# Branch order, interleaved opening of the output projection, and router products of unnormalised tokens in a two-block fp32 kernel

## The reference, cut to what matters

```python
h = rms_norm(x, norm_mix) * (1 + scale_m) + shift_m
proj = h @ w_in
y_a, y_b, y_c = mamba2(...), stick_breaking(...), gated_deltanet(...)      # 256 x 512 each
branch_proj = einsum("bsie,ied->bsid", [y_a, y_b, y_c], w_branch)          # three products, 512 -> 1024
gates = sigmoid(br_gate)                                                   # three slices of proj, 1024 wide
merged = sum(gates * branch_proj, axis=2)
x = x + gate_m * (merged @ w_out)                                          # "the projection" below
h = rms_norm(x, norm_ffn) * (1 + scale_f) + shift_f
logits = h @ [w_group | w_router] + [b_group | b_router]                   # 4 + 32 columns
# top group, then two of its eight experts; SwiGLU experts: (silu(xi @ w_gate) * (xi @ w_up)) @ w_down
x = x + gate_f * hier_moe(h, ...)
```

## Time and profile before

| what | value |
|---|---|
| median of 3 runs | 1608.63 us (1608.3 to 1609.04) |
| the profiled execution | 1611.41 us |
| its span, first to last instruction | 1609.6 us |
| mean granted TensorE clock | 0.96 of full |
| busy: PE, DVE, ACT, POOL | 1499.6, 780.5, 571.4, 294.6 us |
| HBM read | 373.35 MB, 233 GB/s over the span |

### The profile page before, as it was taken

One profiled execution on the slowest core, in us unless ns is written; L12 is line 12 of the kernel. 1 busy time (PEld: TensorE's weight loads), 2 busy tenths in 40 slices (PEclk: granted clock), 3 DMA queues, 4 the chain that ended last, 5 costly groups with the idle time before them and its releaser, 6 DMA issues.

```text
span 1609.6 us, 28268 instructions
## 1 busy us (share of the span) xinstructions
PE 1499.6 (93%) x11238; PEld 1252.1 (78%) x11238; DVE 780.5 (48%) x1411; ACT 571.4 (35%) x895; POOL 294.6 (18%) x121
## 2 busy tenths in 40 slices
PE   7978999999999999999998988978799999999897
PEld 5857999999868999989997977978566665555554
DVE  4963888648674888434543524552422222111212
ACT  2245545454345555356553115433111111101101
POOL 0021112212201212227760002672000000000000
PEclk9989999999999999989999987998899999999999
DMA  7674555664434555625541212463899999999995
GB/s 289 235 275 146 168 169 169 195 235 153 137 134 134 182 185 180 199 92 163 172 144 40 66 40 77 168 239 129 327 424 425 427 428 430 426 427 427 428 427 227
DMA packets 64609, 375.82 MB, mean 233 GB/s; under 512 B 7296, under 2 KB 7552, under 8 KB 49152
## 3 DMA queue, kind: packets, MB, share of 16 engines
q1 hardware_dynamic: 64512, 374.43, 61.9%
HBM read 373.35 MB, written 1.05 MB: 233 GB/s over the span
## 4 chain that ended last, share of the span: by engine, by line
PE 62%; issue 13%; DMA 11%; DVE 8%; SPq 2%; ACT 2%; POOL 1%; POOLq 0%; DVEq 0%; ACTq 0%
PE lin L673 8%; PE lin L675 8%; PE lin L674 8%; DMA modrow<-in_experts 7%; PE mixp L1292 4%; PE mixp L1296 4%; PE stat L1317 4%; DVE mixers L1933 3%; PE lin L692 2%; DMA moe_low<-in_experts 2%; DMA moe_high<-in_experts 2%; DVE cat L2117 1%; PE stat L1260 1%; PE stat L673 1%; PE mixp L673 1%
## 5 line engine op out<-in xcount | busy, mean ns | idle before, releaser
L673 PE MATMUL lin<-r_hi,w_hi 128*128 128x256 f32 x1464 | 428.7, 293 | 14.9 <-POOL w_lo L1737 5.1
L674 PE MATMUL lin<-r_lo,w_hi 128*128 128x256 f32 x1464 | 418.5, 286 | 0.0
L675 PE MATMUL lin<-r_hi,w_lo 128*128 128x256 f32 x1464 | 418.4, 286 | 0.0
L673 PEld LDWEIGHTS lin<-r_hi,w_hi 128*128 128x128 f32 x1464 | 285.4, 195 | 23.0 <-POOL w_lo L1737 6.7
L674 PEld LDWEIGHTS lin<-r_lo,w_hi 128*128 128x128 f32 x1464 | 285.6, 195 | 0.9
L675 PEld LDWEIGHTS lin<-r_hi,w_lo 128*128 128x128 f32 x1464 | 285.2, 195 | 0.0
L1741 POOL TENSOR_TENSOR w_lo<-ring,w_hi 128x1024 fp32r<-128x1024 f32 x71 | 175.4, 2483 | 236.2 <-ACT w_hi L1358 235.8
L1770 DVE TENSOR_TENSOR w_lo<-ring,w_hi 128x1024 fp32r<-128x1024 f32 x126 | 156.5, 1246 | 85.3 <-ACT w_hi L1364 65.2
L1737 POOL TENSOR_TENSOR w_lo<-ring,w_hi 128x1024 fp32r<-128x1024 f32 x42 | 108.3, 2578 | 481.7 <-ACT w_hi L1364 298.4
L1364 ACT ACTIVATE w_hi<-ring 128x1024 fp32r<-128x1024 f32 x124 | 129.6, 1048 | 57.4 <-PE mixp L675 48.5
L1358 ACT ACTIVATE w_hi<-ring 128x1024 fp32r<-128x1024 f32 x119 | 124.0, 1049 | 35.4 <-PE lin L675 17.4
(11 more groups left out here) (460 smaller groups left out, 2834.0 us busy)
## 6 DMA issues: line engine op xcount, KB each, us to landing
ring<-in_panels SPq DMA_DIRECT2D x272, 512.0 KB, 3.6
moe_high<-in_experts SPq DMA_DIRECT2D x32, 2048.0 KB, 30.0
...
```

The costliest lines, as they stand in the source:

```text
L673: pe.matmul(o, w_hi[:, slot, c], r[0], start=start, stop=False, skip_group_check=True)
L674: pe.matmul(o, w_hi[:, slot, c], r[1], start=False, stop=False, skip_group_check=True)
L675: return pe.matmul(o, w_lo[:, slot, c], r[0], start=False, stop=stop, skip_group_check=True)
```

## The change

1. Branch 1 now has the order that branch 0 has: product, gate, gate, four times. `is_gate`, the index of a gate, `gate_branch` and the layout in HBM follow; ACT's `round_merged` calls move among the gates.
2. The projection opens with two panels interleaved tile by tile (`opening`).
3. The router's products use x, not h: `route(m)` multiplies tile m of x with router weights that DVE has scaled by the gain (L2359 of the changed kernel), in [36, 256] form, one in each panel of the projection from the third on. The shift's part is made once by PE (eight products of `mod` broadcast, L1253) and added to the bias row by DVE (L2358). After rs is there, DVE multiplies the 36 x 256 logits by it (L2379), PE turns them with two transposes (L1267), and the routing starts.
4. h is scaled by POOL (x * rs, L1778, eight tiles), ACT applies gain and shift in one operation.
5. Token pieces are turned in the order half 0 of both token tiles, then half 1; the four DVE subtractions stand behind the whole routing instead of in its middle. The fourth bank's zeros come behind the first gathering. `first_max` has one operation less.
6. DVE's `gate_branch(0, 3)` stands ahead of the norm of the gated branch, and ACT splits the second panel of branch 2 behind branch 0's last gates instead of before them.

```diff
@@ -365 +365 @@
-            return j % 3 != 0 if i == BRANCHES[0] else j < KD
+            return j < KD if i == 2 else j % 3 != 0
@@ -492 +492 @@
-        def turn_bank(g):
+        TURNS = ((0, 0), (1, 0), (0, 1), (1, 1))
@@ -494 +494,3 @@
-            return statbank(g - 1) if g in (1, 2) else mixbank(1)
+        def turn_bank(n):
+
+            return (mixbank(1), statbank(0), statbank(1), lin[3][:, :])[n]
@@ -745,0 +748,9 @@
+            def route(m):
+
+                if m == 0:
+                    pe.wait_ge(mod_read, 4)
+                mm = pe.matmul(mixbank(0)[0:36, 0:T], wsmall[:, m, 16:52], x[:, m, :], start=m == 0, stop=m == KD - 1,
+                               skip_group_check=True)
+                if m == KD - 1:
+                    mm.then_inc(ev("logits_ready"), 1)
+
@@ -748 +759,13 @@
-                for m in range(KD):
+                if first:
+                    opening = [split_panel(j) for j in range(2)]
+                    for b in opening:
+                        bank(b)
+                    for i in range(KD):
+                        pe.wait_ge(h_ready, seen(h_ready))
+                        for b in opening:
+                            mm = split_matmul(lin[b][:, 0:T], (b, slice(i * P, (i + 1) * P)), [t[:, i, :] for t in rows],
+                                              i == 0, i == KD - 1)
+                            if i == KD - 1:
+                                mm.then_inc(panel_done, 1)
+                    panels.advance(2)
+                for m in range(2 if first else 0, KD):
@@ -751 +774 @@
-                    split_linear(b, first and m == 0, rows)
+                    split_linear(b, False, rows)
@@ -754,0 +778,2 @@
+                        if first:
+                            route(m - 2)
@@ -756,0 +782,2 @@
+                    if first:
+                        route(m)
@@ -1019 +1046 @@
-                    if split and (i, j) in ((2, 1), (2, KD), (1, KD)):
+                    if split and (i, j) in ((2, 1), (2, KD), (1, 0)):
@@ -1223,0 +1251,5 @@
+            pe.wait_ge(mod_read, 3)
+            for k in range(KD):
+                mm = pe.matmul(mixbank(0)[:, 0:36], mod[:, 3 * KD + k:3 * KD + k + 1].to_broadcast([P, P]), wsmall[:, k, 16:52],
+                               start=k == 0, stop=k == KD - 1, skip_group_check=True)
+            mm.then_inc(mod_turned, 1)
@@ -1229,7 +1260,0 @@
-            for c in range(NT):
-                for i in range(KD):
-                    if c == 0:
-                        pe.wait_ge(h_ready, seen(h_ready))
-                    mm = pe.matmul(mixbank(0)[:, c * 36:(c + 1) * 36], h[:, i, c * P:(c + 1) * P], wsmall[:, i, 16:52],
-                                   start=i == 0, stop=i == KD - 1, skip_group_check=True)
-            mm.then_inc(ev("logits_ready"), 1)
@@ -1238,2 +1263 @@
-            for g in range(4):
-
+            for g in range(3):
@@ -1241,4 +1265,9 @@
-                if g == 3:
-                    pe.wait_ge(ev("ht_copied"), 1)
-                turned(turn_bank(g), [h[:, (g % 2) * 4 + j, (g // 2) * P:(g // 2 + 1) * P] for j in range(4)], ev("ht_turned"))
-            pe.wait_ge(ev("assigned"), 1)
+            pe.wait_ge(ev("routed"), 1)
+            for c in range(NT):
+                mm = pe.transpose(mixbank(0)[:, T + c * 36:T + (c + 1) * 36], e_hid[0:36, c * P:(c + 1) * P], K["ident"][0:36, 0:36])
+            mm.then_inc(ev("logits_ready"), 1)
+            for n, (c, half) in enumerate(TURNS):
+                if n % 2 == 0:
+                    pe.wait_ge(h_ready, seen(h_ready, 4))
+                turned(turn_bank(n), [h[:, half * 4 + j, c * P:(c + 1) * P] for j in range(4)], ev("ht_turned"))
+            pe.wait_ge(ev("routed"), 2)
@@ -1278,0 +1308 @@
+            pe.matmul(lin[3][:, :], e_turned[:, 0:P], cst[:, 0:512], start=True, stop=False, skip_group_check=True)
@@ -1563,2 +1593,4 @@
-                    act.activation(h[:, k, :], h[:, k, :], ACT.Identity, bias=shift)\
-                        .then_inc(r_hi_ready if half == 0 else h_ready, 1)
+                        act.activation(h[:, k, :], h[:, k, :], ACT.Identity, bias=shift).then_inc(r_hi_ready, 1)
+                    else:
+                        act.activation(h[:, k, :], h[:, k, :], ACT.Identity, bias=shift, scale=gains[:, KD + k:KD + k + 1])\
+                            .then_inc(h_ready, 1)
@@ -1587 +1619 @@
-                        u = 2 * (j // 3) + j % 3 - 1 if i == BRANCHES[0] else j
+                        u = j if i == 2 else 2 * (j // 3) + j % 3 - 1
@@ -1664 +1696 @@
-            split_hi(BRANCHES2 + 2)
+            split_hi(BRANCHES2 + 1)
@@ -1682,7 +1714,7 @@
-            gates(1, 0, 10)
-            round_merged(0, 2)
-            gates(1, 10, 11)
-            round_merged(1, 2)
-            gates(1, 11, 12)
-            round_merged(2, 2)
-            round_merged(3, 1)
+            gates(1, 0, 6)
+            round_merged(0, 6)
+            gates(1, 6, 9)
+            round_merged(1, 6)
+            gates(1, 9, 12)
+            round_merged(2, 6)
+            round_merged(3, 3)
@@ -1694 +1726,2 @@
-                act.activation(h_tm_hi[:, g // 2, (g % 2) * 512:(g % 2 + 1) * 512], turn_bank(g), ACT.Copy).then_inc(ev("ht_hi"), 1)
+                c, half = TURNS[g]
+                act.activation(h_tm_hi[:, c, half * 512:(half + 1) * 512], turn_bank(g), ACT.Copy).then_inc(ev("ht_hi"), 1)
@@ -1742,0 +1776,3 @@
+            pool.wait_ge(ev("routed"), 1)
+            for k in range(KD):
+                pool.tensor_tensor(h[:, k, :], x[:, k, :], rs[:, 0, :], ALU.mult).then_inc(ev("h_scaled"), 1)
@@ -2104,2 +2140,2 @@
-                first = i == BRANCHES[0]
-                if not first and pair == 0:
+                in_turn = i != 2
+                if not in_turn and pair == 0:
@@ -2110 +2146 @@
-                    panels.taken(1 + m if first else u - KD - pair)
+                    panels.taken(1 + m if in_turn else u - KD - pair)
@@ -2123 +2159 @@
-                panels.advance(3 if first else 1)
+                panels.advance(3 if in_turn else 1)
@@ -2288,0 +2325 @@
+            gate_branch(0, 3)
@@ -2294 +2330,0 @@
-            gate_branch(0, 3)
@@ -2319,0 +2356,5 @@
+            a0 = ROWS["b_route"][0]
+            dve.wait_ge(mod_turned, 4)
+            dve.tensor_tensor(rows[:, a0:a0 + 36], rows[:, a0:a0 + 36], mixbank(0)[:, 0:36], ALU.add)
+            dve.tensor_tensor(wsmall[:, :, 16:52], wsmall[:, :, 16:52], gains[:, KD:2 * KD].unsqueeze(2).broadcast_to([P, KD, 36]),
+                              ALU.mult).then_inc(mod_read, 1)
@@ -2332,3 +2372,0 @@
-            panels.settled()
-            modulated(KD)
-
@@ -2337,0 +2376 @@
+            panels.settled()
@@ -2339,2 +2378,4 @@
-            a0 = ROWS["b_route"][0]
-            link(dve.tensor_tensor(r_lg, mixbank(0)[:, 0:72].rearrange("p (c n) -> p c n", c=NT),
+            dve.wait_ge(rs_ready, seen(rs_ready))
+            dve.tensor_tensor(e_hid[0:36, :], mixbank(0)[0:36, 0:T], rs[0:36, 0, :], ALU.mult).then_inc(ev("routed"), 1)
+            dve.wait_ge(ev("logits_ready"), 2)
+            link(dve.tensor_tensor(r_lg, mixbank(0)[:, T:T + 72].rearrange("p (c n) -> p c n", c=NT),
@@ -2356,2 +2397 @@
-                link(dve.tensor_scalar(r_at, r_at, 1000.0, None, ALU.add))
-                link(dve.tensor_tensor(onehot, iota(n), wide(r_at, n), ALU.is_equal))
+                link(dve.tensor_tensor(onehot, onehot, wide(r_at, n), ALU.is_equal))
@@ -2362 +2402 @@
-                c, d = g // 2, slice((g % 2) * 512, (g % 2 + 1) * 512)
+                c, d = TURNS[g][0], slice(TURNS[g][1] * 512, (TURNS[g][1] + 1) * 512)
@@ -2369,2 +2408,0 @@
-            for g in range(3):
-                lower_tokens(g)
@@ -2385,3 +2423,4 @@
-            dve.tensor_tensor(assign, r_oh1, r_oh2, ALU.add).then_inc(ev("assigned"), 1)
-            lower_tokens(3)
-            dve.wait_ge(ev("assigned"), 1)
+            dve.tensor_tensor(assign, r_oh1, r_oh2, ALU.add).then_inc(ev("routed"), 1)
+            for g in range(4):
+                lower_tokens(g)
+            dve.wait_ge(ev("routed"), 2)
@@ -2497 +2536 @@
-        if i == 0:
+        if i != 2:
```

## The result

The changed kernel takes 1597.33 us in the median of 8 runs (1586.21 to 1599.94), the kernel before 1608.84 in 8 runs (1599.1 to 1610.95): ratio 0.993, 95% interval 0.9902 to 0.9957. That is 11.5 us less; 9.8 were forecast.

What follows compares the result with a forecast made beforehand. The DMA stream of expert weights bounds the last stage, so its start and holes set the end. Closing the hole (-7.7 us) and an earlier projection end (-2.05) gave -9.8: 1598.8 us, range 1594.5 to 1604.8.

Steps and rivals of the forecast that it cites:

- hole: Expert weight stream runs dry before expert 3's load, which waits for step 0; sized 7.7 us, forecast to close.
- (a) to (c): Up to branch 2's merges: PE stall removed, shift products added, router-weight scaling delays merges; together +1.3 us (-0.6 to +1.7).
- (d): Branch 1's new order: product banks come free slightly late at three places; +0.6 us (0 to 2.6).
- (e): PE's 7.39 us idle time between branch 1 and the projection shrinks; -5.5 us (-5.9 to -4.2).
- (f): Opening of the projection: first panel no longer slowed by the lower PE clock; -1.5 us.
- (g): Five router products on PE before the projection's last panel, 0.43 us each; +2.15 us.
- (h): Projection's first two panels end together, so the fourth panel's split is late; +0.9 us (0 to 1.8).
- The room: Step 0 reads its weights 32.5 us behind the projection's end, up to 36.5 with POOL/DVE contention; limit 37.5.
- 1: Rival: POOL slows both chains behind rs, step 0 through at +40 to +41.5; 2.5 to 4 us stall remains; 1602; chance 0.09.
- 2: Rival: PE's wait before the projection stays, last merges or c_hi still ending 7 us behind the products; 1605.9; chance 0.07.
- 4: Rival, slower: POOL's h tiles cost by the instruction, stream stalls 13.5 us instead of 7.7; 1612.4; chance 0.04.
- 3: Rival, more gained: no POOL-slowed scaling, no lower clock, no late fourth-panel split; projection -6 us; 1594.9; chance 0.10.

Runs made afterwards that it cites:

- seam_only: Kernel before with only branch 1 in the order product, gate, gate and the two-panel opening of the projection; 1598.99 us, ratio 0.9958 to the kernel before.
- routes_behind: Changed kernel with router products moved behind the projection's last sums and three banks' zeros placed among the turned tokens; 1585.45 us.

## Why the prediction came out as it did

**Right in kind.** The forecast's case came in: hole closed, seam shorter. By steps, forecast against measured, for the end of the projection:

| step | forecast | measured | from |
|---|---|---|---|
| (a) to (c) | +1.3 | +0.6 | opening, changed less seam_only |
| (d) | +0.6 | +0.2 | end of branch 1, seam_only less before |
| (e) | -5.5 | -5.7 | 7.39 against 1.66 |
| (f) | -1.5 | -1.9 | opening to stream, 27.05 against 28.18, less (h) |
| (g) | +2.15 | +3.0 | routes_behind |
| (h) | +0.9 | +0.8 | wait ahead of the fourth panel in seam_only |
| sum | -2.05 | -3.1 | stream |

The first two lines are at the size of the scatter of 0.5 us. That the sum is only 1.0 off is in part luck: (a) to (c) were forecast 0.7 too long and (g) 0.85 too short.

**(a) to (c).** The chain was right: y1's lower part comes 1.1 us earlier, then 0.18 for the bias and 2.55 for the scaling beside POOL (forecast 0.23 and 2.1), first merge 1.5 later. But it was carried through to the end at its full size, and only part arrived. In seam_only the merges start 1.86 us earlier than in the changed kernel, but the first five additions fall beside POOL and the first ten take 16.2 us; in the changed kernel two fall into POOL's pause and ten take 15.0. Of the 1.86 us 1.2 are won back there, and 0.6 arrive. The fourth panel of branch 1 was to come later than 1052.43: it came at 1052.30, from the mark 0.13 later.

**(g)** was mis-sized. A router product was priced as a sum over x, 0.43 us, and cost 0.75. From sum to sum a panel takes 4.05 us after (1097.89 to 1101.94 above), and before, in PE's order of time:

```profile
1096.84 0.59 PE L712 MATMUL stat<-sq,cst 128*128 128x256 f32 x2
...
1100.14 0.59 PE L712 MATMUL stat<-sq,cst 128*128 128x256 f32 x2
```

That is 3.30, so 0.75 more. Four such products are 3.0. The fifth, the first in time, lies in the wait for the fourth panel (h) and is free: 0.22 us of idle time are left of 0.78. The two steps share their place, and the prediction added them.

**The hole** was mis-sized: it was read as 7.7 us from the DMA share; by bytes it is 9.7, and 9.5 came back. The share of 0.88 over 1158 to 1165 went with 316 GB/s, so it should not have been taken at its face. This one term is most of what the total was short: 1.8 of 2.8 us from the mark.

**The room** was thought to be 5 us (32.5 against 37.5) and was 1.2 (33.9 against 35.1, both behind the projection's end). The forecast stood closer to the edge than it said: with its own 32.5 there would have been 2.6 us to spare, not 5, and the upper bound of its own contention term, +36.5, would have left 1.4 us of hole. That the hole closed whole was thus less certain than its "both ends lie below 37.5".

**Behind the projection**, +33.9 against +32.5. The tiles were 0.69 us each (guess 0.8), h was whole with ACT's part at +11.9 (+12.2). The routing took 8.44 us instead of 5.7: operations of 0.2 us take 0.45 to 0.74 there beside POOL's tiles, as the rows from 1118.70 on show, 2.7 us in all. The prediction had allowed for that with 4 us in its upper bound. That chain, not the tokens, ended last: PE's ranks wait for DVE's row at 1124.83, and the idle time ahead of them is 1.07.

**Rivals.** 1 and 2 are out by the traces. 4 is out: POOL's tile costs by its elements, a quarter of 2.48 plus 0.07. 3 came close in size, 12.5 us against its 13.7, but not by its path: the projection gave 3.1 of its 6, and the rest is the mis-sized hole. Of its three reasons one held, the clock; the slot in (c) and the wait of (h) were both there.
